# An RWKV layer whose sixth step carries three projection halves and whose seventh carries two

## The chip, the cores and the metric

One core of one Trainium2 chip runs the whole program. The metric is device time in microseconds, the median of several runs. A profile of one execution gives the trace. TensorE (PE in the rows) does matrix products, VectorE (DVE), ScalarE (ACT) and GpSimd (POOL) do elementwise work, SyncE (SP) issues loads.

## The reference, cut to what matters

Two transformer-like blocks run over 512 tokens of width 1024. The first has dilated attention beside an RWKV-7 time mix, then a feed-forward part; the second block is of another kind and isn't touched. What matters is the time mix:

```python
h = rmsnorm(x, norm_mix_pre[l])
proj = h @ w_in[l]
f_att, f_rwkv, f_gate = jnp.split(proj, [3 * ATT_WIDTH, 3 * ATT_WIDTH + RWKV_COLS], axis=-1)
...
def step(state, inp):
    r_t, w_t, k_t, v_t, kk_t, a_t = inp
    sa = jnp.einsum('bhij,bhj->bhi', state, -kk_t)
    state = (state * w_t[:, :, None, :]
             + sa[..., None] * (kk_t * a_t)[:, :, None, :]
             + v_t[..., None] * k_t[:, :, None, :])
    y_t = jnp.einsum('bhij,bhj->bhi', state, r_t)
    return state, y_t
...
gates = jax.nn.sigmoid(f_gate + b_gate[l]).reshape(b, s, N_BRANCHES, D_MODEL)
merged = (gates[:, :, 0] * (o_att @ w_att_branch[l])
          + gates[:, :, 1] * (o_rwkv @ w_rwkv_branch[l]))
```

The columns of r, k and v (1024 each), the low-rank inputs and the two gates (1024 each) are all products of the same normed input with `w_in`; they don't depend on the recurrence.

## The kernel before

**The steps.** The 16 heads are worked on as 8 pairs. The recurrence over 512 tokens is done in 4 chunks of 128 tokens, and each chunk needs the inverse of a triangular matrix, made in levels by doubling its blocks. The program runs eight steps, `step(0)` to `step(7)`, called the first to the eighth here. Step p works on three pairs at once: pair a = p (the chunks: right-hand side, solve, output), pair b = p + 1 (the inverse, levels 1 to 6, then Gram products and a refinement) and pair c = p + 2 (its preparation: decay, key norm, rates, queries). So the sixth step, `step(5)`, has pairs 5, 6 and 7, and the seventh, `step(6)`, has pairs 6 and 7 and no third one.

**The level chain of pair b.** A level goes from PE (line 1116) to ACT, which copies the result (line 1762), to PE again (line 1128, two groups), to DVE, which copies it under a mask (line 2589) and masks it (line 2591, `tinv`), to PE for the next level. All these are in-order queues written out by hand, and engines wait for each other by semaphores.

**The projection halves.** To cover the waits of these chains, PE's queue holds products that depend on nothing in them: the remaining columns of `w_in`. A half is 128 columns (of a weight unit of 256) times all 512 tokens: 8 pieces of three products of 128x512 (lines 654 to 656; the weights and inputs are split into a high and a low part). `HALVES` lists 42 halves in order; `STEP_HALVES` gives each step up to three of them, the first, the middle and the last. `fill()` puts the next pieces into PE's queue, as many as the next entry of the step's slots says:

```python
SLOTS3 = (1, 1, 2, 1, 1, 1, 1, 0, 1, 1, 1, 1, 1, 2, 1, 1, 1, 2, 1, 1, 2)
SLOTS2 = (1, 1, 2, 1, 1, 1, 1, 0, 0, 0, 0, 0, 1, 1, 1, 1, 1, 1, 0, 0, 2)
...
slots = iter(SLOTS_LAST if p == 7 else SLOTS2 if None in STEP_HALVES[p] else SLOTS3)
```

So a step with a None has 16 pieces and the others 24, and in a step of two halves the slots from the third chunk's start to the fourth level are empty. All these halves use one PSUM bank, so a half can't start until the one before has been taken out of it.

**Who takes a half.** Halves 33 to 35 are r, k and v of pair 7: ACT copies them (line 1591) and DVE shifts them by a token (line 2491). Halves 36 to 41 are columns of the second gate: ACT applies a Sigmoid (line 1602) into a work tile that pair 7 no longer needs, and stores it to DRAM (line 1604). The one of half 36, into `sig_w`, waits until DVE has made the queries of pair 7 (line 2530), and that of half 37, into `cum_decay`, until DVE has made its keys (line 2548, the last DVE work of the sixth step). In ACT's queue, the first half of a step is taken behind the right-hand side of the third chunk; the middle half behind the copies of the tokens, ahead of the root of the variance (line 1818); the last half at the start of the next step, behind its first right-hand side. ACT needs another function table (ACT_TABLE_LOAD) when it goes between Exp, Sigmoid and Sqrt; a Sigmoid's table is loaded at the end of each step (line 1676).

**Weights.** A unit holds two neighbouring halves. SP loads the units into a ring of three, each as soon as the unit three before it has been used; ACT makes the high part (line 1472), DVE the low part (line 2479). In which step they do so depends on which odd-numbered half is a step's first, middle or last.

Of the kernel before, what the change touches and what calls it, by code (L numbers as in the profile page):

```python
# [64 lines left out]
HALF = {what: n for n, what in enumerate(HALVES)}  # L65
N_SHIFTED = [sum(what[0] in ("lora", "rkv") for what in HALVES[:n + 1]) for n in range(len(HALVES))]

STEP_HALVES = {-1: (None, None, 19), 5: (35, None, 36), 6: (37, 38, 39), 7: (40, 41, None)}
STEP_HALVES.update({p: (20 + 3 * p, 21 + 3 * p, 22 + 3 * p) for p in range(5)})

FIRST_HALVES = range(12, 20)
# [144 lines left out]
def build(nc, x, wpack, lora_wa, lora_g, params, rel_bias, post_gains, sink, ctab, btab, icount, out):  # L216
# [8 lines left out]
    with ExitStack() as ctx:  # L225
# [423 lines left out]
        def _(pe):  # L649
# [356 lines left out]
            def step_halves(p):  # L1006
                for n in STEP_HALVES[p]:
                    if n is not None:
                        yield from side_half(n, half_bank(n), n - 2 if n in LAST_BANKS or n - 1 in LAST_BANKS else n - 1)
# [271 lines left out]
            def step(p):  # L1281
# [3 lines left out]
                halves = step_halves(p)  # L1285
                slots = iter(SLOTS_LAST if p == 7 else SLOTS2 if None in STEP_HALVES[p] else SLOTS3)

# [175 lines left out]
        def _(act):  # L1463
# [443 lines left out]
            def step(p):  # L1907

                a, b, c = p, p + 1, p + 2
                has_b, has_c = b < PAIRS, c < PAIRS  # L1910
                first, middle, _ = STEP_HALVES[p]
                last = STEP_HALVES[p - 1][2]
                gate_last = HALVES[last][0] != "rkv"
# [310 lines left out]
        def _(dve):  # L2224
# [489 lines left out]
            def step(p):  # L2714

                a, b, c = p, p + 1, p + 2
                has_b, has_c = b < PAIRS, c < PAIRS
                first, middle, _ = STEP_HALVES[p]
                before, last = STEP_HALVES[p - 1][1:]
# [334 lines left out]
```

## Time and profile before

| | |
|---|---|
| median of 3 runs | 1761.08 us (1760.17 to 1761.31) |
| the profiled execution | 1761.03 us |
| its span, first to last instruction | 1759.2 us |
| PE busy | 1738.5 us, 99% |
| DVE, ACT, POOL busy | 839.6, 724.5, 503.0 us |
| granted clock of TensorE | 0.999 of full speed |

An engine is busy while an instruction of its own runs; a wait is idle time ahead of an instruction. Matrix products overlap, so the start of one to the start of the next is what one costs in a row of them. All times in the rows are in us from the start of the span. A row of the timeline gives start, duration, engine, line, operation, output and inputs, how many were merged, and, in brackets, idle time ahead of it and what ended that.

### The profile page before, as it was taken

The numbers are of one execution on the slowest core, as the hardware profiler recorded it, in microseconds if no ns is written. First come the engines' busy times: TensorE is split into PE (matmuls) and PEld (weight loads), VectorE is DVE, ScalarE is ACT, GpSimd is POOL, SyncE is SP. The second block draws the span as 40 slices with busy tenths as digits, with TensorE's granted clock in tenths as the row PEclk, the third lists the DMA queues.
The fourth block names the chain that finished last, engine by engine and source line by source line (L and its number), as shares of the span: only waits on it lengthen the run. The fifth ranks groups of instructions, "written<-read, shape, count | busy, mean of one in ns | idle before, by whom it ended". The sixth has DMA issues, their size and how long they took to land.

```text
span 1759.2 us, 22211 instructions
## 1 busy us (share of the span) xinstructions
PE 1738.5 (99%) x9392; PEld 1436.4 (82%) x9392; DVE 839.6 (48%) x1195; ACT 724.5 (41%) x1092; POOL 503.0 (29%) x126
## 2 busy tenths in 40 slices
PE   9999999999999999999999999999999999999998
PEld 8898778888888888888888888877778888888887
DVE  3015477998989754251124443627844411123343
ACT  5244555655566452352232223536652522222222
POOL 2442300000000003524444444233344244444442
PEclk9999999999999999999999999999999999999999
DMA  5432231110011124432222222322222222222221
GB/s 199 165 125 72 93 99 57 28 52 25 28 39 38 37 104 148 143 108 96 96 96 96 96 96 96 115 87 72 73 96 96 93 100 101 100 97 96 96 96 72
DMA packets 57238, 159.46 MB, mean 91 GB/s; under 512 B 3471, under 2 KB 35087, under 8 KB 42548
## 3 DMA queue, kind: packets, MB, share of 16 engines
q1 hardware_dynamic: 45132, 137.64, 22.8%
q10 hardware_dynamic: 12008, 20.40, 3.4%
q8 instruction: 75, 1.23, 0.3%
q14 instruction: 23, 0.19, 0.0%
HBM read 150.41 MB, written 9.19 MB: 91 GB/s over the span
## 4 chain that ended last, share of the span: by engine, by line
PE 91%; DVE 4%; ACT 3%; DMA 1%; issue 1%; POOL 0%; ACTq 0%; SPq 0%; DVEq 0%
PE ps L654 26%; PE ps L656 24%; PE ps L655 24%; PE ps L1128 2%; PE ps L1213 1%; PE ps L1116 1%; ACT ht_hi L1507 1%; PE ps L1171 1%; PE ps L1136 1%; DMA w_raw<-in_wpack 1%; PE ps L1045 1%; PE ps L1161 1%; PE ps L840 1%; PE ps L1181 1%; PE ps L873 1%
## 5 line engine op out<-in xcount | busy, mean ns | idle before, releaser
L645 POOL TENSOR_TENSOR w_lo<-w_raw,w_hi 128x2048 fp32r<-128x2048 f32 (+2 forms) x122 | 502.8, 4127 | 1229.3 <-ACT w_hi L1472 1206.8
L654 PE MATMUL ps<-ht_hi,w_hi 128*128 128x512 f32 (+1 forms) x1312 | 524.6, 400 | 3.7 <-DVE ht_lo L2252 3.4
L656 PE MATMUL ps<-ht_hi,w_lo 128*128 128x512 f32 (+1 forms) x1312 | 499.6, 381 | 0.0
L655 PE MATMUL ps<-ht_lo,w_hi 128*128 128x512 f32 (+1 forms) x1312 | 498.8, 380 | 0.0
L1472 ACT ACTIVATE w_hi<-w_raw 128x2048 fp32r<-128x2048 f32 x125 | 239.3, 1915 | 453.7 <-PE ps L656 400.6
L654 PEld LDWEIGHTS ps<-ht_hi,w_hi 128*128 128x128 f32 x1312 | 247.4, 189 | 63.7 <-issue 18.0
L656 PEld LDWEIGHTS ps<-ht_hi,w_lo 128*128 128x128 f32 x1312 | 247.1, 188 | 48.7
L655 PEld LDWEIGHTS ps<-ht_lo,w_hi 128*128 128x128 f32 x1312 | 247.8, 189 | 39.4 <-issue 1.9
L2853 DVE TENSOR_TENSOR hid_lo<-hidden,hid_hi 128x1024 fp32r<-128x1024 f32 x27 | 129.3, 4788 | 149.1 <-ACT hid_hi L2050 149.1
L654 PE MATMUL ps<-w_hi,hid_hi 128*128 128x512 f32 x432 | 168.2, 389 | 0.0
L656 PE MATMUL ps<-w_hi,hid_lo 128*128 128x512 f32 x432 | 168.1, 389 | 0.0
L655 PE MATMUL ps<-w_lo,hid_hi 128*128 128x512 f32 x432 | 168.1, 389 | 0.0
L656 PEld LDWEIGHTS ps<-w_hi,hid_lo 128*128 128x128 f32 x432 | 81.1, 188 | 16.9
L654 PEld LDWEIGHTS ps<-w_hi,hid_hi 128*128 128x128 f32 x432 | 81.1, 188 | 16.7
L655 PEld LDWEIGHTS ps<-w_lo,hid_hi 128*128 128x128 f32 x432 | 81.1, 188 | 16.7
L2863 DVE TENSOR_TENSOR hidden<-ps,gate_act 128x1024 f32<-128x1024 f32 x16 | 19.6, 1225 | 128.5 <-ACT gate_act L2089 128.5
L654 PE MATMUL ps<-w_hi,ht_hi 128*128 128x512 f32 (+1 forms) x224 | 77.5, 346 | 0.3 <-DVEq L2838 0.2
L656 PE MATMUL ps<-w_hi,ht_lo 128*128 128x512 f32 (+1 forms) x224 | 77.1, 344 | 0.0
L655 PE MATMUL ps<-w_lo,ht_hi 128*128 128x512 f32 (+1 forms) x224 | 77.0, 344 | 0.0
L2589 DVE COPY_PREDICATED inverse<-consts,ps 128x512 f32<-128x512 int32 x80 | 58.4, 730 | 23.9 <-PE ps L1128 23.5
L2089 ACT ACTIVATE gate_act<-ps 128x1024 f32<-128x1024 f32 x16 | 16.5, 1029 | 121.8 <-PE ps L656 121.8
L2955 DVE TENSOR_TENSOR hidden<-ps,hidden 128x1024 f32<-128x1024 f32 x11 | 13.5, 1225 | 95.3 <-PE ps L656 95.3
(354 smaller groups left out, 2353.1 us busy)
## 6 DMA issues: line engine op xcount, KB each, us to landing
w_raw<-in_wpack SPq DMA_DIRECT2D x113, 1024.0 KB, 4.8
w_raw<-in_wpack SPq DMA_DIRECT2D x26, 512.0 KB, 5.2
x_res<-in_x SPq DMA_DIRECT2D x4, 512.0 KB, 6.2
gate_back<-gate_dram ACTq DMA_DIRECT2D x2, 1024.0 KB, 6.7
gate<-gate_dram ACTq DMA_DIRECT2D x1, 2048.0 KB, 8.5
x_res<-in_x ACTq DMA_DIRECT2D x1, 2048.0 KB, 7.9
bias_skewed_dram<-bias_rows_dram ACTq DMA_DIRECT2D x1, 1792.0 KB, 10.5
gate_dram<-rwkv_out ACTq DMA_DIRECT2D x6, 256.0 KB, 3.5
```

The costliest lines, as they stand in the source:

```text
L645: last = nc.gpsimd.tensor_tensor(Wl[:, slot, cc], raw[:, slot, cc], f32(Wh[:, slot, cc]), ALU.subtract)
L654: mm(dst, wh, ah, start=first, stop=False)
L655: mm(dst, wh, al, start=False, stop=False)
L656: return mm(dst, wl, ah, start=False, stop=last)
L840: last = mm(bank(4 + h, it["n"]), it["q"][h], it["k"][h], start=True, stop=True)
L873: last = mm(ps[it["rows"][h], 7, 0:P], v, PT2[h][:, j, :], start=j == 0, stop=j == len(it["vals"]) - 1)
L1045: last = mm(dst[:, 2 * t:2 * t + 2], src[:, tok(t)], root_cols(ones_head), start=True, stop=True)
L1128: last = mm(ps[:, (4, 6)[k], tok(t)], (tt, x)[k], (x, tt)[k], start=True, stop=True)
L1472: actf(Wh[:, n % RING, :], raw[:, n % RING, :], ACT.Copy).then_inc(hi_ready, 1)
L2589: order(v.copy_predicated(Wf[k][:], blocks(lv - 1), src))
L2853: v.tensor_tensor(HIl[:, 2 * g:2 * g + 2, :], HID[:, 2 * g:2 * g + 2, :], f32(HIh[:, g % RING, :, :]), ALU.subtract).then_inc(hid_lo, 1)
L2863: v.tensor_tensor(HID[:, 2 * u:2 * u + 2, :], ps[:, 2 * (d % 2):2 * (d % 2) + 2, :], SG[:], ALU.mult).then_inc(pair_taken[d % 2], 1)
```

## The change

Half 36, the third gate half, moves from the last place of the sixth step to its middle place, 37 from the first place of the seventh to the last of the sixth, and 38 from the middle of the seventh to its first place. Since a None decides the list of slots, the sixth step goes from `SLOTS2` to `SLOTS3` and the seventh from `SLOTS3` to `SLOTS2`. The order of the halves, and what is computed, stays the same.

```diff
-STEP_HALVES = {-1: (None, None, 19), 5: (35, None, 36), 6: (37, 38, 39), 7: (40, 41, None)}
+STEP_HALVES = {-1: (None, None, 19), 5: (35, 36, 37), 6: (38, None, 39), 7: (40, 41, None)}
 STEP_HALVES.update({p: (20 + 3 * p, 21 + 3 * p, 22 + 3 * p) for p in range(5)})
```

The high and low parts of the units are made at the same places of the queues as before.

## Rows read from the trace of the kernel before

**Rows 1.** The page: busy time and share of each engine.

```profile
PE 1738.5 (99%) x9392; PEld 1436.4 (82%) x9392; DVE 839.6 (48%) x1195; ACT 724.5 (41%) x1092; POOL 503.0 (29%) x126
```

**Rows 2.** Busy time by window: the fifth, sixth and seventh step.

```profile
491.69:542.39 50.70, 50.40 (x353) 41.69 (x352) 44.65 (x81) 30.82 (x53) 0.00 (x0) 1.00 0.15 43
542.39:589.92 47.53, 46.00 (x334) 37.97 (x333) 44.53 (x79) 28.55 (x51) 0.00 (x0) 1.00 0.08 23
589.92:636.51 46.59, 46.37 (x338) 39.97 (x336) 33.36 (x58) 20.22 (x38) 0.00 (x0) 1.00 0.13 41
```

**Rows 3.** Timeline of PE, sixth step: first products of a level.

```profile
562.17 0.63 PE L1116 MATMUL ps<-tinv,level 128*128 128x128 f32 x4 [0.16 <-DVE tinv L2591]
...
571.93 0.64 PE L1116 MATMUL ps<-tinv,level 128*128 128x128 f32 x4 [0.46 <-DVE tinv L2591]
```

**Rows 4.** Timeline of PE, seventh step: a piece, then the refining product.

```profile
630.02 0.39 PE L654 MATMUL ps<-ht_hi,w_hi 128*128 128x512 f32 x1
...
630.70 1.95 PE L1136 MATMUL ps<-tinv,gram_inv 128*128 128x128 f32 x16
```

**Rows 5.** Timeline of PE: values transposed (fifth step), centred (seventh).

```profile
518.59 0.62 PE L1203 MATMUL ps<-consts,rkv 128*128 128x128 f32 x4
...
614.45 1.11 PE L1201 MATMUL ps<-consts,rkv 128*128 128x128 f32 x8
```

**Rows 6.** Timeline of DVE, fifth step: fifth level's copy, reciprocal of the root.

```profile
520.78 0.74 DVE L2589 COPY_PREDICATED inverse<-consts,ps 128x512 f32<-128x512 int32 x1 [0.22 <-PE ps L1128]
...
528.65 0.19 DVE L2640 RECIPROCAL root<-root 128x8 f32<-128x8 f32 x1
```

**Rows 7.** Timeline of DVE, sixth step: fifth level's copy, queries, keys.

```profile
570.32 0.74 DVE L2589 COPY_PREDICATED inverse<-consts,ps 128x512 f32<-128x512 int32 x1
...
575.20 0.69 DVE L2530 SCALAR_TENSOR_TENSOR ra<-kk,work_t 128x512 f32<-128x512 f32 x1
...
590.32 0.69 DVE L2548 TENSOR_TENSOR kb<-rkv,work_x 128x512 f32<-128x512 f32 x1
```

**Rows 8.** Timeline of ACT, fifth step: tokens, a load, the activation behind it.

```profile
524.08 0.59 ACT L1823 ACTIVATE b_chunk<-ps 128x512 f32<-128x512 f32 x1
...
538.33 1.28 ACT L1754 ACT_TABLE_LOAD   x1
540.32 0.63 ACT L1754 ACTIVATE work_x<-work_e 128x512 f32<-128x512 f32 x1 [0.71 <-PE ps L1074]
```

**Rows 9.** Timeline of ACT, seventh step: a gate's Sigmoid and the load behind.

```profile
620.90 0.69 ACT L1602 ACTIVATE kk<-ps,params_sb 128x512 f32<-128x512 f32 x1
...
621.97 1.28 ACT L1818 ACT_TABLE_LOAD   x1 [0.39 <-ACT kk L1602]
```

**Rows 10.** Timeline of PE, fifth step: a piece, spreading products.

```profile
527.02 0.53 PE L654 MATMUL ps<-ht_hi,w_hi 128*128 128x512 f32 x1
...
530.47 0.60 PE L1051 MATMUL ps<-consts,norm_sq 128*128 128x128 f32 x4
```

**Rows 11.** Timeline of PE, seventh step: a piece, three levels, last Grams.

```profile
591.96 0.48 PE L654 MATMUL ps<-ht_hi,w_hi 128*128 128x512 f32 x1
...
608.50 0.56 PE L1116 MATMUL ps<-tinv,level 128*128 128x128 f32 x4
...
614.05 0.56 PE L1116 MATMUL ps<-tinv,level 128*128 128x128 f32 x4
...
618.79 0.57 PE L1116 MATMUL ps<-tinv,level 128*128 128x128 f32 x4
...
632.58 0.70 PE L1213 MATMUL ps<-ra,kb 64*128 64x256 f32 x4
```

**Rows 12.** Timeline of DVE, seventh step: head Gram, level copy, Gram copy.

```profile
610.01 0.69 DVE L2598 TENSOR_TENSOR gram_inv<-gram_inv,sides 128x512 f32<-128x512 f32 x1
...
617.12 0.74 DVE L2589 COPY_PREDICATED inverse<-consts,ps 128x512 f32<-128x512 int32 x1 [2.72 <-PE ps L1128]
...
631.55 0.58 DVE L2627 COPY_PREDICATED gram<-consts,ps 128x384 f32<-128x384 int32 x1
```

## The prediction

> **What bounds the kernel now.** I read the page's busy line first: TensorE (PE) is busy for 1738.5 us of a 1759.2 us span [rows 1]. About 21 us in the whole kernel are therefore not PE work, and a reordering of products can only move those. The profiled execution took 1761.03 us, 1.83 more than its span; the median of the three runs, 1761.08, is the same within their spread, so a change of the span is added to 1761.03.
>
> Next I cut the span at the first product of each step (line 1161 with its four products) and read the stages. The fifth step takes 50.70 us, the sixth 47.53 and the seventh 46.59 [rows 2]. The fifth has three halves and work of all three pairs. The sixth has only two halves, with work of three pairs; the seventh three halves, with no third pair. The granted clock is 1.00 in all three. The idle part (window less PE busy) is 0.30, 1.53 and 0.22 us: the sixth step is the one with holes. The timeline of PE shows where: at the first product of a level (line 1116), which waits for DVE's masked tile `tinv` [rows 3]; three such waits stand from 562.17 to 571.93, just where its slots hold no pieces.
>
> **The change, part by part.** Eight pieces (one half) leave the seventh step and enter the sixth. Half 36 is now the middle half of the sixth step, 37 its last, 38 the first of the seventh; the list of slots of the two steps is exchanged. Nothing is computed more or less, so the sum is: what the sixth grows by, less what the seventh shrinks by.
>
> A piece costs 0.68 us in a row of pieces (630.02 to 630.70) [rows 4], so a half is 8 x 0.68 = 5.4 us. Without waits the two terms would cancel at 5.4.
>
> *The sixth step.* It now has the slots of the fifth, which took 50.70 us with the same pairs at work. One thing differs: from pair 6 on, the values are centred by eight products at line 1201 (1.11 us) where the fifth step transposes them with four at line 1203 (0.62) [rows 5]: +0.48. I take 50.70 + 0.48 = 51.18, that is **+3.65 us** on 47.53. So of 5.4 us of added products 1.8 fall into the present holes.
>
> This supposes that the middle half does no harm, and it is another kind of half: in the fifth step a projection half, which ACT copies and DVE shifts; now a gate half, a Sigmoid on ACT into `sig_w`, which waits for DVE's queries of pair 7 (they read `sig_w`). In the fifth step's clock, 0.48 added for the centring: DVE starts the fifth level at 520.78 + 0.48 = 521.26, as soon as PE lets it [rows 6]. From that point to the end of the queries the sixth step takes 575.20 + 0.69 - 570.32 = 5.57 (the key norm stands in between there) [rows 7]: 526.83. ACT is free of `b_chunk` at 524.67 + 0.48 = 525.15 [rows 8], and its table must change from Exp to Sigmoid, 1.28: done at 526.43, before the queries. The Sigmoid runs from 526.88 to 527.57 (0.69 [rows 9]). PE reaches the first piece of half 37, which needs that bank, at 527.02 + 0.48 = 527.50 [rows 10]: a wait of 0.1, which is below what this sum can resolve, and I put it at nothing.
>
> Queued behind the Sigmoid on ACT is the root of the variance, with a table load of its own. In the seventh step that load starts 1.07 after the start of a Sigmoid (620.90 to 621.97, its store issued in between) [rows 9]: here 527.95. Load 1.28, root 0.19 (taken as long as DVE's reciprocal of the same eight columns [rows 6], an estimate), reciprocal 0.19, widening 0.63 (as the ACT row of 128x512 at 540.32 [rows 8]), 0.2 for handing over: 530.44. PE wants it for the spreading products at 530.47 + 0.48 = 530.95 [rows 10]. So it is hidden by pieces and products with 0.5 in hand; what exceeds that costs one for one.
>
> One thing is not shown: whether the load of a table runs ahead of the wait. With one wait it does: the load at 538.33 ran long before the wait ended at 540.32 [rows 8]. The Sigmoid has two waits. If its load stood behind them, everything from there would be 1.28 later: PE would wait 1.4 at the first piece. That bounds this term: nothing to 1.4; I take nothing, by the row with one wait.
>
> The Trainium skill ("ScalarE: Activation LUTs", section "What ACT_TABLE_LOAD costs") speaks against this edit: it counts 1283 ns for the load and some 1380 ns of drain, 2.66 us in all, for each switch to another set, and would have calls batched by set. The load agrees with the row, the drain has no row here; by its 2.66 the root path would end near 532.75, 1.8 late, and the sum would be 1763.5 where the rows give 1761.7 (an estimate by that page).
>
> *Into the seventh step.* Half 37 is taken at its start, behind `rhs`, and waits for the last DVE work of the sixth step, `keys`, which ended at 591.01 [rows 7]. Its Sigmoid would run from 591.06 to 591.75; PE starts the next half at 591.96 [rows 11]. That leaves 0.2, so no cost, and one for one beyond it. The loads on SP's queue keep their order; the unit behind halves 36 and 37 is freed half a step earlier, at a DMA share of 0.08 [rows 2]. ACT's store of a gate moves with its Sigmoid and is counted above.
>
> *The seventh step.* It loses the pieces of four slots around the third and fourth level, one of two behind the fourth level's products, and three near the end. Is that time won, or do the products wait?
>
> Third to fourth level. Four pieces go, one ahead of 608.50 and three between 608.50 and 614.05 [rows 11]. PE could start the fourth level at 614.05 - 4 x 0.68 = 611.33. But DVE's two head Grams stand in its queue until 610.70 [rows 12], released by products that ran before any removed piece, so they do not move. The copy and mask behind them take 1.61 to the product they release (570.32 [rows 7] to 571.93 [rows 3]); starting at 610.65, as the Grams drain, they release the level at 612.26. Won 614.05 - 612.26 = 1.79 of 2.7.
>
> Fourth to fifth. From 614.05 to DVE's copy at 617.12 [rows 11, 12] nothing changes: 3.07. So the copy is at 615.33, the product at 616.94 against 618.79: won 1.85 so far, of five pieces (3.4). Up to line 1136 all shifts by 1.85.
>
> Near the end. Two pieces ahead of the refining product (630.70 [rows 4]) go: 627.49. But the last Gram products wait for DVE's Gram copy, done at 631.55 + 0.58 = 632.13 [rows 12], which moves only by 1.85, to 630.28. They start at 630.33, not 632.58 [rows 11]: won 2.25. The last removed piece stands behind them: 0.7 more. **The seventh step shrinks by 2.95 us**, to about 43.6.
>
> **Sum:** +3.65 - 2.95 = +0.70 us, 1761.03 + 0.70 = **1761.7 us**. The holes are not filled, they move: 1.8 us of them vanish in the sixth step and 2.5 (5.4 - 2.95) appear in the seventh. 0.2% of this kernel is 3.5 us; my sum is a fifth of that, so I forecast no change that can be told.
>
> **Rivals.**
> 1. *The seventh step has slack enough.* If the pieces removed there covered nothing, it would shrink by 5.4: +3.65 - 5.4 = -1.75, 1759.3. For it: in that step DVE waits 2.72 for PE ahead of its copy [rows 12], so PE is late, not DVE. Against it: that wait is shorter than the pieces removed between two levels. The half-way case is 1760.5.
> 2. *The Sigmoid's load waits in the sixth step*: +1.4, 1763.1. For it: two waits; against: the row with one.
> 3. *Slower than before: the level chain is the floor of the seventh step.* If the chain from level to level is already as long as the step, removing pieces only opens holes, the seventh step stays at 46.59 and the sixth's +3.65 stands alone: 1764.7, just over 0.2%. It decides if the first products of the fourth to sixth level keep their distances, 5.55 and 4.74 us [rows 11]. Against it: DVE waits for PE there [rows 12], and a level without pieces is shorter: 1.61 on DVE plus the products.
> 4. *Each change of table holds ACT for longer than its row.* If it held it for twice the 1.28, the Sigmoid would start at 527.71 instead of 526.88 and the root path end at 527.71 + 1.07 + 2.56 + 1.21 = 532.55, 1.6 after PE wants it: 1763.3. Against it: between a Sigmoid's end and the end of the load behind it there stand only the store and the load (620.90 + 0.69 to 621.97 + 1.28) [rows 9]. This is the rule of the page named above.
>
> **Chances.** Forecast (+0.2 to +1.3) 0.60; rival 1, in whole or half, 0.17; rival 2 0.12; rival 3 0.05; rival 4 0.03; the rest, of either sign, 0.03. The forecast's own range, with the 1.1 us by which the three runs differ, is 1760.9 to 1762.6. For 8 in 10 it must reach into rivals 1 and 2: 1759.6 to 1763.5. Faster by over 0.2% (below 1757.5) has no mechanism, as the holes in both steps are 1.75 us in all: 0.02. Slower by over 0.2% needs rival 3, or 2 and 4 together: 0.05. Within 0.2%: 0.93.
>
> **What would show it.** In the profile after: the sixth step near 51.2 us, with no wait for `tinv` at line 1116; the seventh near 43.6, with such waits of up to 1 us at the fourth and fifth level and one for DVE's Gram copy at line 1213; one table load more in the sixth step, its Sigmoid starting as the queries end, and the load ahead of that; the eighth step unchanged. I am wrong if the sixth step exceeds 52 (rival 2 or 4), or the seventh is below 42.5 (rival 1) or above 45 (rival 3).

## The result and the profile after

The changed kernel takes 1765.3 us (median of 7 runs, 1763.15 to 1769.25) against 1761.08 for the kernel before (7 runs): a ratio of 1.0026, with a 95% interval of 1.0016 to 1.0036. The forecast was 1761.7, in a range of 1759.6 to 1763.5. The time is outside it, slower than was foreseen, and just past the 0.2% that can be told from no change.

The profiled execution took 1765.3 us, with a span of 1763.5. The same cut at the first product of each step gives these windows (duration; busy time of PE, PEld, DVE, ACT, POOL; granted clock, DMA share, GB/s), for the fifth, sixth and seventh step, as in [rows 2]:

```profile
491.90:542.61 50.71, 50.41 (x354) 41.71 (x352) 44.66 (x81) 30.80 (x53) 0.00 (x0) 1.00 0.15 43
542.61:597.50 54.89, 53.54 (x358) 44.45 (x357) 45.20 (x79) 30.61 (x53) 0.00 (x0) 0.94 0.09 25
597.50:641.27 43.77, 41.45 (x313) 35.79 (x312) 32.93 (x58) 19.72 (x37) 0.00 (x0) 1.00 0.11 38
```

The seventh step shrank by 2.82 (2.95 was forecast). The sixth grew by 7.36 where 3.65 was forecast; the whole miss is there. Look at its clock too: 0.94, where each of the three steps had 1.00 before. What follows the seventh step took 1122.7 before and 1122.2 after: none of the miss is there.

PE's timeline of the sixth step shows where it is lost, around the first piece of half 37:

```profile
578.17 0.39 PE L1215 MATMUL ps<-ra,kb 64*128 64x128 f32 x4
579.87 0.79 PE L654 MATMUL ps<-ht_hi,w_hi 128*128 128x512 f32 x1 [1.31 <-ACT sig_w L1602]
...
581.32 0.95 PE L1116 MATMUL ps<-tinv,level 128*128 128x128 f32 x4
...
585.92 0.64 PE L1128 MATMUL ps<-xinv,tinv_t 128*128 128x128 f32 x4
```

Two things are to be seen. The piece waits 1.31 us for the Sigmoid of half 36. And the products behind the hole are slow: four level products take 0.95, against 0.64 in [rows 3]. From the piece to the next product of line 1128 PE needs 585.92 - 579.87 = 6.05 us with no idle time in it. Windows ahead of the hole, in it, behind it and later say why:

```profile
570.00:578.17 8.17, 8.13 (x58) 7.07 (x58) 6.70 (x12) 5.87 (x11) 0.00 (x0) 1.00 0.00 0
578.17:579.87 1.70, 0.39 (x6) 0.19 (x3) 1.67 (x5) 1.64 (x2) 0.00 (x0) 0.77 0.00 0
579.87:585.92 6.05, 6.05 (x22) 4.85 (x23) 2.79 (x7) 2.66 (x4) 0.00 (x0) 0.50 0.13 46
585.92:590.00 4.08, 4.08 (x27) 3.25 (x25) 3.22 (x5) 1.51 (x4) 0.00 (x0) 1.00 0.00 0
```

Behind the hole the granted clock is 0.50, the 1.2 GHz level, until 585.92; then it is 1.00 again.

Why the Sigmoid is late is on ACT's timeline:

```profile
575.49 0.59 ACT L1823 ACTIVATE b_chunk<-ps 128x512 f32<-128x512 f32 x1
577.84 1.28 ACT L1602 ACT_TABLE_LOAD   x1 [1.76 <-DVE ra L2530]
579.13 0.69 ACT L1602 ACTIVATE sig_w<-ps,params_sb 128x512 f32<-128x512 f32 x1
...
580.21 1.28 ACT L1818 ACT_TABLE_LOAD   x1 [0.39 <-ACT sig_w L1602]
```

ACT is free at 575.49 + 0.59 = 576.08, but the load of the Sigmoid's table comes 1.76 later, when DVE's queries are done. In ACT's queue of the built program the two waits written ahead of the Sigmoid are in different places. The one written last, for the queries (`ra_ready`), is an instruction of its own ahead of the load; the load has no wait; the other, for the half (`side_full`), stays on the activation:

```
L1599 EVENT_SEMAPHORE                           [waits ra_ready]
L1602 ACT_TABLE_LOAD
L1602 ACTIVATE sig_w<-ps,params_sb 128x512      [waits side_full]
```

The working in terms, by the distance from each step's start: in the fifth step of the kernel before the piece stands at 527.02 - 491.69 = 35.33 [rows 10], here at 579.87 - 542.61 = 37.26. Of the 1.93 between them 0.48 is the centring that was forecast and **1.31 is the hole**, by its row; the other 0.14 is there without the hole too (0.13 in experiment 5). The stretch from the piece to line 1128 is 6.05 here; the same stretch is 3.63 in experiment 3 (six products), with the piece as late and the clock at 1.00, so **the clock costs about 2.4**. Forecast 3.65, 1.31 and 2.42 make 7.38; measured 7.36.

### The profile page after: what moved, and what is told of

Same layout as the page of the kernel before. It is cut to its first block, busy times and chain, and to the rows that moved or that the text cites. A ratio compares the mean times of both kernels' runs of the same rounds, so it can differ in the third digit from the quotient of the medians.

```text
span 1763.5 us, 22212 instructions
## 1 busy us (share of the span) xinstructions
PE 1739.0 (99%) x9392; PEld 1438.3 (82%) x9392; DVE 840.1 (48%) x1195; ACT 725.3 (41%) x1093; POOL 502.8 (29%) x126
## 3 DMA queue, kind: packets, MB, share of 16 engines
q8 instruction: 75, 1.23, 0.3%
## 4 chain that ended last, share of the span: by engine, by line
PE 90%; DVE 5%; ACT 3%; issue 1%; DMA 0%; ACTq 0%; SPq 0%; DVEq 0%
PE ps L654 25%; PE ps L656 24%; PE ps L655 24%; PE ps L1128 2%; PE ps L1116 1%; PE ps L1213 1%; PE ps L1171 1%; ACT ht_hi L1507 1%; PE ps L1045 1%; PE ps L1136 1%; PE ps L1161 1%; PE ps L840 1%; DVE ht_lo L2252 1%; PE ps L1181 1%; PE ps L873 1%
```

## The experiments

The theory (A): the load stands behind the queries' wait, this opens the hole, and the clock's fall behind the hole is the rest; nothing else in the forecast is wrong. Against it stood that a switch of tables holds ACT for more than its row, that the third half in the sixth step costs more for another reason (its gate half, its store, the added products), and that the slow products have nothing to do with the hole.

**1. The load ahead of the waits.** The changed kernel, with a Sigmoid on one column, which waits for nothing, in front of the middle half, so that the table is there early:

```diff
                 if p < 7:
+                    if p == 5:
+                        table(ACT.Sigmoid)
                     take_half(middle)
```

> The changed kernel, but a Sigmoid on one column, which waits for nothing, stands in ACT's queue right ahead of half 36 in the sixth step, so that the table is loaded while ACT would wait for the queries. Theory A (the load stands behind the wait, PE's hole of 1.31 us comes from that, and the clock falls because of the hole): the load runs from about 576.1, the Sigmoid starts within 0.1 us of the end of the queries, no hole over 0.3 us ahead of half 37, granted clock 1.00, sixth step 51.2 to 51.6 us, time 0.6 to 1.2 us above before, 1761.7 to 1762.3. Rival B (two table switches in the middle of the step hold up ACT's root path, wherever the load stands): sixth step above 53 us, time above 1763.5. Rival C (the clock falls there for another reason than the hole): granted clock 0.5 for some us again, time about 1764.

Measured: 1762.33 us (11 runs) against 1761.14: 1.0008 (0.9999 to 1.0016). The sixth step is 51.21 at a clock of 1.00. The seventh is 45.42 in this profile, and not for the load: there the hole that was forecast ahead of the fourth level is followed by a fall of the clock (PE's timeline, then windows of the sixth step, of the seventh and of the stretch behind the hole).

```profile
617.35 0.68 PE L1116 MATMUL ps<-tinv,level 128*128 128x128 f32 x4 [0.67 <-DVE tinv L2593]
617.83 2.02 PE L1201 MATMUL ps<-consts,rkv 128*128 128x128 f32 x8
```

```profile
543.83:595.04 51.21, 50.93 (x358) 42.31 (x356) 45.02 (x79) 30.82 (x54) 0.00 (x0) 1.00 0.09 26
595.04:640.46 45.42, 43.12 (x313) 37.34 (x312) 32.94 (x58) 19.83 (x37) 0.00 (x0) 0.96 0.10 36
...
617.83:621.20 3.37, 3.37 (x16) 3.27 (x16) 0.71 (x2) 1.66 (x3) 0.00 (x0) 0.50 0.00 0
```

The eight products take 2.02 instead of 1.11 [rows 5]. The hole in the sixth step hung on the load's place alone; and a fall can follow a hole in another place.

**2. The hole alone, in the kernel before.** The kernel before, with no half moved; in the sixth step PE waits at the same place for DVE's reciprocal of the root, which it needs only later:

```diff
                     grams(b, 0)
+                if p == 5:
+                    w("rv_ready", 1, a, 1)
                 fill()
```

> The kernel before, but in the sixth step PE waits for DVE's reciprocal of the root ahead of the same slot (the first behind the fifth level's second products), which makes a hole of about 1.7 us at 576.6 with no gate half and no table load near it. Theory A (a hole of that length is what lets the clock fall): granted clock 0.5 for some us behind it, sixth step 47.5 + 1.7 + 2 or so = 51, time 3 to 4 us above before. Rival C (the clock falls for another reason, such as the table loads or what ACT does): clock 1.00, sixth step about 49, time 1 to 1.7 us above before.

Measured: 1765.23 us (8 runs) against 1761.14: 1.0025 (1.0015 to 1.0035), as much as the whole change. The first two lines are PE's timeline, the last two windows of the sixth step and of the stretch behind the hole:

```profile
577.96 0.50 PE L654 MATMUL ps<-ht_hi,w_hi 128*128 128x512 f32 x1 [1.68 <-DVE root L2642]
...
578.98 0.95 PE L1116 MATMUL ps<-tinv,level 128*128 128x128 f32 x4
```

```profile
541.99:593.91 51.92, 49.03 (x333) 40.63 (x332) 44.87 (x79) 28.79 (x51) 0.00 (x0) 0.93 0.07 21
...
578.46:585.30 6.84, 6.84 (x29) 5.77 (x28) 2.49 (x6) 1.27 (x4) 0.00 (x0) 0.50 0.01 2
```

With a hole of 1.68 the step is 51.92 - 47.53 = 4.39 longer; the clock stood at 0.50 for some 6.8 us behind it. Neither the gate's Sigmoid nor its table load is there: here the hole is enough.

**3. The hole filled with idle products.** The changed kernel, as late as it is, but PE multiplies a constant tile into an unused bank in front of the piece, first twelve times, then six (the added products are no part of the reference):

```diff
                     grams(b, 0)
+                if p == 5:
+                    for _ in range(6):
+                        mm(ps[:, 7, 0:P], ident, ident, start=True, stop=True)
                 fill()
```

> The changed kernel, but twelve idle products of 128x128 on the identity (about 0.11 us each, into an unused bank) stand in PE's queue of the sixth step ahead of the first piece of half 37, where the hole of 1.31 us is. They only keep PE at work while it waits. Theory A: the wait stays (first piece at about 579.9 as in the changed kernel), but the clock stays at 1.00, so the stretch to the sixth level's second products takes 3.8 instead of 6.05 us: sixth step about 52.6, time 2.2 us below the changed kernel, about 1763. Rival E (these products are slow for another reason, such as ACT and DVE on the same banks, and the clock has no part): sixth step 54.9, time as the changed kernel, 1765.

Twelve: 1764.34 us (11 runs) against 1761.14, 1.0019 (1.0009 to 1.0028). The sixth step is 53.46, its clock 1.00. This met its aim in part (about 52.6 and 1763 had been expected): twelve products took 581.59 - 578.88 = 2.71 us and put the piece at 38.60 from the step's start, 1.3 later than in the changed kernel. Behind them the slow products were gone (581.59 to 584.86, 3.27). So six were run:

> The changed kernel with six idle products ahead of the first piece of half 37 (twelve took 2.71 us, so six take 1.35, as long as the hole). Theory A: first piece where the changed kernel has it (37.3 us into the step), clock 1.00, the stretch from there to the sixth level's second products 3.3 to 3.8 instead of 6.05 us, sixth step 52.1 to 52.6, time 2.3 to 2.8 us below the changed kernel, 1762.5 to 1763. Rival E (the products behind the hole are slow for another reason than the clock): sixth step 54.9, time 1765.

Six: 1762.75 us (11 runs) against 1760.99, 1.0010 (1.0001 to 1.0019). PE's timeline and the window of the sixth step:

```profile
577.60 1.60 PE L1349 MATMUL ps<-consts 128*128 128x128 f32 x12
578.98 0.50 PE L654 MATMUL ps<-ht_hi,w_hi 128*128 128x512 f32 x1
...
579.79 0.56 PE L1116 MATMUL ps<-tinv,level 128*128 128x128 f32 x4
...
582.61 0.64 PE L1128 MATMUL ps<-xinv,tinv_t 128*128 128x128 f32 x4
```

```profile
541.71:594.18 52.47, 52.35 (x369) 43.68 (x368) 45.00 (x79) 30.62 (x53) 0.00 (x0) 1.00 0.09 26
```

The piece stands at 578.98 - 541.71 = 37.27, as in the changed kernel (37.26): just as late. But PE did not idle, the clock stayed at 1.00, and the step is 54.89 - 52.47 = 2.42 shorter. That separates the two costs: the lateness is about 1.3 (52.47 - 51.16, next), the clock 2.4. The medians agree: this kernel stands 1.76 above the kernel before, the changed kernel 4.22 and, measured again below, 4.48.

**4. No wait for the queries.** The Sigmoid of half 36 writes a tile that is free by then (a quarter of `rwkv_out`, once its earlier store is done), so that its wait for the queries falls away:

```diff
-buf = ORW[:, 4 + u, :] if u < 2 else (SZ, CS, KK, E, T1, X2)[u - 2][:]
+buf = ORW[:, 4 + u, :] if u < 2 else ORW[:, 7, :] if u == 2 else (CS, KK, E, T1, X2)[u - 3][:]
 act.wait_ge(side_full, n + 1)
-if u == 2:
-    act.wait_ge(rs["ra_ready"], PAIRS)
-elif u == 3:
+if u == 3:
...
+                if p == 6:
+                    act.wait_ge(gate_stored, 16 * 3)
```

> The changed kernel, but half 36 goes into the still unused eighth row of the tile of outputs instead of the work tile, so that its Sigmoid does not wait for the queries (ACT waits for the store at the start of the seventh step). Theory A (the table load stands behind the wait for the queries): with that wait gone the load runs right behind b_chunk, the Sigmoid about 1 us earlier than with the load put ahead by hand, no hole ahead of half 37, granted clock 1.00 in the sixth step, sixth step 51.1 to 51.3 us, time 0.4 to 1.4 us above before (more where the clock falls in the seventh step). Rival B (two table switches in the middle of the step are the cost): sixth step above 53, time above 1763.5.

Measured: 1761.73 us (11 runs) against 1760.99: 1.0005 (0.9996 to 1.0014). With one wait, which stays on the activation, the load runs right behind the tokens, as the row with one wait [rows 8] had it (ACT's timeline, its line numbers two lower, then the window of the sixth step):

```profile
574.97 0.59 ACT L1821 ACTIVATE b_chunk<-ps 128x512 f32<-128x512 f32 x1
575.58 1.28 ACT L1600 ACT_TABLE_LOAD   x1
576.87 0.69 ACT L1600 ACTIVATE rwkv_out<-ps,params_sb 128x512 f32<-128x512 f32 x1
```

```profile
542.08:593.24 51.16, 50.84 (x358) 42.23 (x357) 44.97 (x79) 30.63 (x53) 0.00 (x0) 1.00 0.09 26
```

The sixth step is 51.16, the seventh 43.76. All the rest of the change is in this kernel, so the third half in the sixth step costs what was forecast (51.18).

**5. The two waits in the other order.** The smallest edit: the changed kernel, with both waits kept and `side_full` written last.

```diff
-act.wait_ge(side_full, n + 1)
 if u == 2:
     act.wait_ge(rs["ra_ready"], PAIRS)
 elif u == 3:
     act.wait_ge(rs["kb_ready"], PAIRS)
+act.wait_ge(side_full, n + 1)
```

> The changed kernel with nothing but the two waits ahead of the gate's Sigmoid written in the other order: first the wait for the queries (or keys), then the one for the half. In the program as compiled the table load then carries the wait for the half and the Sigmoid the one for the queries; in the changed kernel it is the other way round. Theory A: the load runs right behind b_chunk, as half 36 is done by then, the Sigmoid starts as the queries end, PE waits 0.1 to 0.3 us at most, clock 1.00 in the sixth step, sixth step 51.1 to 51.4 us, time 0.5 to 1.2 us above before, and 3 below the changed kernel. Rival G (the load waits for all that the Sigmoid waits for, whatever the order): as the changed kernel, sixth step 53 to 55, time 1764 to 1766.

Measured: 1761.8 us (11 runs) against 1761.06: 1.0005 (0.9996 to 1.0014). In the built program the two waits have changed places: the one ahead of the load is for `side_full`, which came early, the one on the activation for `ra_ready`. (The expectation says that the load carries a wait; it is an instruction of its own in front of the load, and in a queue worked off in order that comes to the same.) ACT's timeline, the first piece of half 37 on PE's, and the windows of the sixth and seventh step:

```profile
575.75 1.28 ACT L1602 ACT_TABLE_LOAD   x1
577.45 0.69 ACT L1602 ACTIVATE sig_w<-ps,params_sb 128x512 f32<-128x512 f32 x1 [0.42 <-DVE ra L2530]
...
578.53 1.28 ACT L1818 ACT_TABLE_LOAD   x1 [0.39 <-ACT sig_w L1602]
...
580.37 0.63 ACT L1733 ACTIVATE norm_sq<-root 128x512 f32<-128x512 f32 x1 [0.27 <-DVE root L2640]
```

```profile
578.19 0.50 PE L654 MATMUL ps<-ht_hi,w_hi 128*128 128x512 f32 x1
```

```profile
542.25:593.41 51.16, 50.86 (x357) 42.23 (x356) 45.02 (x79) 30.61 (x53) 0.00 (x0) 1.00 0.09 26
593.41:637.19 43.78, 41.47 (x313) 35.76 (x312) 32.94 (x58) 19.76 (x37) 0.00 (x0) 1.00 0.11 37
```

Only the order of the waits differs from the changed kernel. The wait for the queries still holds the Sigmoid, for 0.42, but behind the load, and the piece starts with no wait. With it the hole, the slow clock and 3.7 us are gone (1765.54 for the changed kernel beside it, below).

**6. The switch of tables alone.** The kernel before, with the Sigmoid on one column ahead of the root in the sixth step: a load there and a load back, and nothing of the change.

```diff
+                    if p == 5:
+                        table(ACT.Sigmoid)
                     take_half(middle)
```

> The kernel before, but in the sixth step ACT does a Sigmoid on one column behind the third copy of the tokens, ahead of the root: two table loads in a row with no gate half and no wait. Theory A: the root comes 1.5 us later, at about 577.0, still ahead of DVE's reciprocal at 578.1, so the sixth step stays at 47.5 and the time at that of before, within 0.3 us. Rival B (a switch holds ACT for longer than its row, by a drain of its own): the root comes 4 us later or more, the spreading products are late, sixth step above 49.

Measured: 1760.58 us (10 runs) against 1760.99: 0.9998 (0.9989 to 1.0007). ACT's timeline and the window of the sixth step:

```profile
574.31 0.59 ACT L1823 ACTIVATE b_chunk<-ps 128x512 f32<-128x512 f32 x1
574.92 1.28 ACT L1676 ACT_TABLE_LOAD   x1
576.21 0.20 ACT L1676 ACTIVATE stat<-consts 128x1 f32<-128x1 f32 x1
576.42 1.28 ACT L1818 ACT_TABLE_LOAD   x1
577.72 0.27 ACT L1818 ACTIVATE root<-ps,consts 128x8 f32<-128x8 f32 x1
```

```profile
543.10:590.62 47.52, 46.02 (x334) 37.97 (x333) 44.51 (x79) 30.02 (x53) 0.00 (x0) 1.00 0.08 23
```

Two loads and the activation between them take 577.72 - 574.92 = 2.80, which is 2 x 1.28 + 0.20 and 0.04 between the rows; the first load starts 0.02 behind the copy of the tokens (574.31 + 0.59). So these rows show no idle time beside a load, and the sixth step stays at 47.52: an added switch is hidden there.

**7. The seventh step's products spread anew.** From the kernel of experiment 1, the two halves of the seventh step are its middle and its last, with slots of their own, so that pieces stand where the holes were:

```diff
-... 6: (38, None, 39), ...
+... 6: (None, 38, 39), ...
+SLOTS7 = (1, 0, 1, 1, 0, 1, 0, 0, 0, 1, 0, 1, 0, 1, 1, 1, 1, 2, 1, 1, 2)
```

> The changed kernel with the table loaded ahead of the wait, and in the seventh step half 38 as the middle half with slots of its own (1, 0, 1, 1, 0, 1, 0, 0, 0, 1, 0, 1, 0, 1, 1, 1, 1, 2, 1, 1, 2): fewer pieces early, eight behind the fifth level as in the kernel before. Theory A (the seventh step loses what it loses because pieces lack at the late levels and ahead of the last Gram products, while early ones cover nothing): no hole for DVE's Gram copy, seventh step 41.9 to 42.5 instead of 43.8, sixth 51.2, time 0.3 to 1 us below before, 1760.2 to 1760.8. Rival F (the early pieces cover waits as well): holes among the first levels, seventh step 43.5 to 45, time 1761.5 to 1763.

Measured: 1761.62 us (11 runs) against 1760.99: 1.0003 (0.9994 to 1.0012). The step is 43.32, 0.45 shorter than in the changed kernel, but not the 41.9 to 42.5 of theory A: rival F is nearer. The hole at the Gram products is gone, others came (the window of the seventh step, then PE's timeline, its line numbers one higher):

```profile
593.97:637.29 43.32, 41.42 (x313) 35.67 (x312) 33.35 (x58) 19.53 (x37) 0.00 (x0) 1.00 0.11 38
```

```profile
600.79 0.66 PE L1117 MATMUL ps<-tinv,level 128*128 128x128 f32 x4 [0.53 <-ACT level L1780]
...
606.56 0.49 PE L1160 MATMUL ps<-state,ra 128*128 128x128 f32 x2 [0.68 <-DVE state L2624]
...
619.51 0.63 PE L1117 MATMUL ps<-tinv,level 128*128 128x128 f32 x4 [0.46 <-DVE tinv L2594]
```

With 16 pieces the chains show through wherever the pieces don't stand. This beats neither the kernel before nor the kernels of experiments 4 and 5 by more than can be told.

**8. The changed kernel again**, beside the kernel of experiment 5.

> The changed kernel itself, beside the swapped waits on one chip. Theory A: the hole of 1.3 us is there in every run, and 1763.2 is what it costs without a fall of the clock (0.7 forecast + 1.4 of hole); runs whose mean granted clock is lower are longer, by some 2 us for each fall: median 1764.5 to 1766 and clocks of 0.996 to 0.998. Rival H (the seven runs shown were taken on an unlucky chip): median 1762 to 1763.

Measured: 1765.54 us (11 runs) against 1761.06: 1.0024 (1.0016 to 1.0033). The hole is the same to the hundredth, the fall behind it is shorter (PE's timeline, then windows of the sixth step and of the stretch behind the hole):

```profile
582.37 0.77 PE L654 MATMUL ps<-ht_hi,w_hi 128*128 128x512 f32 x1 [1.31 <-ACT sig_w L1602]
```

```profile
545.10:598.83 53.73, 52.36 (x357) 43.54 (x356) 45.19 (x79) 30.61 (x53) 0.00 (x0) 0.97 0.09 25
...
582.37:586.00 3.63, 3.63 (x15) 3.01 (x15) 1.74 (x4) 2.67 (x4) 0.00 (x0) 0.53 0.22 77
```

The step is 53.73, 1.16 less than in the first profile, and 1.26 more than with the hole filled (52.47). The hole is as long in both profiles, the clock's part is not. That this execution, at 1766.79, is still the longer of the two comes from ahead of the sixth step, which begins 2.49 later in it. Two of the eleven runs, with a mean clock of 0.999 and 1.0 over the whole kernel, took 1762.19 and 1762.13; the other nine, at 0.996 to 0.998, took 1764.08 to 1767.43. Of the first seven runs, however, the one with a mean clock of 1.0 took 1763.99.

## Why the prediction was wrong, point by point

**The step that failed.** "One thing is not shown: whether the load of a table runs ahead of the wait. [...] That bounds this term: nothing to 1.4; I take nothing, by the row with one wait." With two waits the load stood behind one of them, and it was the late one. That is rival 2, which had a chance of 0.12. Its price for the hole was right: 1.4 was given, and the hole measured 1.31. The place of the miss was seen, and the wrong end of the bound taken: the row cited had one wait, the Sigmoid two. The sign given for it, a sixth step over 52, came up with 54.89.

**The term that was missing.** Rival 2 gave 1763.1; the kernel took 1765.3. The rest is the clock, about 2.4 us in the profile, which the prediction reads as "1.00 in all three" and then leaves out: each hole was priced by its own length. So a time slower by over 0.2% was to need "rival 3, or 2 and 4 together" and got a chance of 0.05; rival 2 alone, with the clock, did it. Experiments 2 and 3 show both directions: a hole without the change brings the fall, the change without the idle time does not. The trace of before had shown such a fall, in a step that I did not read. The first two lines are PE's timeline of the second step, the last two windows of it, in the kernel before:

```profile
228.16 0.40 PE L656 MATMUL ps<-ht_hi,w_lo 128*128 128x512 f32 x1
230.68 0.37 PE L1101 MATMUL ps<-ra,kb 64*128 64x128 f32 x1 [2.12 <-DVE kb L2544]
```

```profile
228.00:231.00 3.00, 0.88 (x7) 0.44 (x7) 3.00 (x4) 1.54 (x2) 0.00 (x0) 1.00 0.19 73
231.00:235.00 4.00, 4.00 (x24) 3.23 (x21) 3.62 (x6) 0.49 (x1) 0.00 (x0) 0.63 0.03 11
```

A hole of 2.12 stood ahead of a clock of 0.63. With that row in hand, the upper bound of rival 2 would have been higher by the cost of a fall, and the range with it.

**What was right.** With the order of the waits mended (experiment 5) every other term can be compared. The sixth step: 51.18 forecast, 51.16 measured. On ACT, in that run's clock (50.56 later than the fifth step of before), the Sigmoid was forecast for 526.88, that is 577.44, and started at 577.45; the next load for 578.51, and started at 578.53; the root path was to end at 581.00, and did, at 580.37 + 0.63. That last agreement is in part luck: the root took 0.27 where 0.19 was put, and the 0.2 for handing over, for which no row was given, came to less than 0.1. DVE's queries were right in the changed kernel too: 577.75 forecast (50.92 later), 577.76 measured. Half 37 at the start of the seventh step cost nothing.

The seventh step, in the changed kernel, has its three holes where they were forecast (PE's timeline):

```profile
619.80 0.63 PE L1116 MATMUL ps<-tinv,level 128*128 128x128 f32 x4 [0.67 <-DVE tinv L2591]
...
624.54 0.64 PE L1116 MATMUL ps<-tinv,level 128*128 128x128 f32 x4 [0.45 <-DVE tinv L2591]
...
637.97 0.70 PE L1213 MATMUL ps<-ra,kb 64*128 64x256 f32 x4 [0.88 <-DVE gram L2627]
```

Counted from the step's start against [rows 11], the fourth level is 1.83 earlier (1.79 forecast), the fifth 1.83 (1.85), the Gram products 2.19 (2.25), the end 2.82 (2.95). Experiments 4 and 5 repeat it (43.76, 43.78). With experiment 5 the sum of the moved work is 3.63 - 2.81 = +0.82 where +0.70 was forecast, and the kernels of experiments 4 and 5 are +0.74 above the kernel before in their medians, each alone no more than can be told from nothing.

**A price that was off.** A half was priced at 5.4 us, 0.68 for a piece. By the windows [rows 2] and those of experiment 5, PE's busy time grew by 50.86 - 46.00 = 4.86 in the sixth step and fell by 46.37 - 41.47 = 4.90 in the seventh, 0.61 for a piece. So 1.23 us of idle time went in the sixth step (1.53 to 0.30), not 1.8, and 2.09 came in the seventh (0.22 to 2.31), not 2.5. It hardly shows in the sum, as the sixth step was taken from the fifth and not from the price of pieces.

**The rivals.** Rival 1 (slack in the seventh step) and rival 3 (the chain as its floor) fall with 43.77: neither 41.2 nor 46.6. Of the two distances that rival 3 names (they are those of the third to the fifth level, not of the fourth to the sixth), 5.55 became 619.80 - 615.28 = 4.52, and 4.74 stayed (624.54 - 619.80). Experiment 7 tried one other list of places for the pieces; it gained 0.45. Rival 4, the drain of the Trainium skill ("ScalarE: Activation LUTs", "What ACT_TABLE_LOAD costs"), falls with experiment 6. That page's 1283 ns for the load agrees with the rows (1.28); its 1380 ns of drain is in none of them, and here the measurement decides. The skill's 1763.5 came nearer to the measured time than the forecast, by a cause that is not there.

**What stays open.** Why the clock falls behind some holes and not behind others is not settled. The holes of 0.45 to 0.88 in the seventh step left it at 1.00 in the changed kernel and in experiments 3 to 5, and 0.67 was followed by a fall in experiment 1. The hole of 2.1 in the second step was followed by a fall in the profile of before, not in those of experiments 1, 4 and 5. Even the same program shows both: in the first profile of the changed kernel the clock stayed at 1.00 behind that hole (2.11; windows from 231 to 240), in the second it fell (2.16, with one of 1.29 ahead of it; 0.73 from 235 to 240). Whether some run of the changed kernel kept its clock behind the hole of 1.31 was not seen in a profile; the two runs of 1762.1 and 1762.2 suggest it, but do not show it.

## What to carry to other kernels

Where an activation changes the table and has more than one wait, look in the built program which wait stands ahead of the load, and write the late one so that it stays on the activation: here that was the one written first, and the order alone was worth 3.7 us. Price a hole in PE's queue not by its length only, but also by what the granted clock does behind it, and look for a hole of that kind anywhere in the trace of before. Of a bound "nothing to 1.4", take the end whose row has the same form, and where no row has it, keep the far end in the forecast.

## What the runs showed of the hardware that was not expected

- A hole of 1.31 us between stretches in which PE is busy throughout was followed by the 1.2 GHz level for 6.05 us in one profile (clock 0.50) and 3.6 in another (0.53), one of 1.68 by some 6.8 us, one of 0.67 by 3.4. The cost, about 2.4 and 1.3 us in the two profiles of the changed kernel, is about as large as the hole or larger.
- Idle products in the hole kept the clock at 1.00 and shortened the step by 2.42 us. Six of them took 578.98 - 577.60 = 1.38 us, 0.23 each; in the trace each counts as two products.
- The Trainium skill ("TensorE: Matmul & The Clock Gate", "What's actually happening") says that the gate follows how busy PE has been of late. The runs agree in kind; that the same hole is followed by falls of different length is in the two profiles above.
